# Attention transposes one turn after the scaling of their probabilities, in the turn of two interleaved scans that had no attention work

## What is computed

```python
s = (jnp.einsum('bqhd,bkhd->bhqk', qn_b, k_nope)
     + jnp.einsum('bqhd,bkd->bhqk', qr_b, k_rope))
p = jax.nn.softmax(s.astype(jnp.float32) * scale, axis=-1)
return jnp.einsum('bhqk,bkhd->bqhd', p.astype(v.dtype), v)
```

## Time and profile before

| | |
|---|---|
| median of 3 executions | 3255.03 us |
| profiled execution | 3253.55 us |
| its span | 3251.3 us |
| TensorE busy | 3132.6 us, 96% |
| VectorE, ScalarE, GpSimd busy | 64%, 41%, 29% |
| stretch with scans and attention | 531 to 1140 us |
| TensorE busy from 570 to 1128 us | 527.8 of 558.0 us |

### The profile page before, as it was taken

One profiled execution on the slowest core, in us unless ns is written; L12 is line 12 of the kernel. 1 busy time (PEld: TensorE's weight loads), 2 busy tenths in 40 slices (PEclk: granted clock), 3 DMA queues, 4 the chain that ended last, 5 costly groups with the idle time before them and its releaser, 6 DMA issues.

```text
span 3251.3 us, 62204 instructions
## 1 busy us (share of the span) xinstructions
PE 3132.6 (96%) x26688; PEld 2561.6 (79%) x26688; DVE 2084.1 (64%) x3018; ACT 1343.6 (41%) x2442; POOL 937.5 (29%) x810
## 2 busy tenths in 40 slices
PE   8999998999999988999999999999999999999998
PEld 8678776887788777787888888878677878888887
DVE  5263465666766665856999778752555575655686
ACT  4333334555555444533433344442332343333444
POOL 1232243222222142501576640000000025666100
PEclk9999999999999999999999999999999999999999
DMA  4241245112112122552222347422002312322753
GB/s 152 68 155 52 72 158 169 56 42 64 64 45 63 54 82 71 165 191 79 94 104 97 110 159 247 158 96 93 33 27 96 131 68 101 107 101 98 268 159 117
DMA packets 128018, 346.48 MB, mean 107 GB/s; under 512 B 15792, under 2 KB 19520, under 8 KB 124928
## 3 DMA queue, kind: packets, MB, share of 16 engines
q1 hardware_dynamic: 106592, 258.09, 23.8%
q0 software_dynamic: 21152, 84.42, 7.0%
HBM read 246.51 MB, written 95.94 MB: 105 GB/s over the span
## 4 chain that ended last, share of the span: by engine, by line
PE 84%; DVE 9%; ACT 4%; issue 2%; POOL 1%; DMA 1%; SPq 0%; DVEq 0%; ACTq 0%; POOLq 0%
PE ps L378 41%; PE ps L377 39%; PE ps L381 3%; DVE AR L387 2%; DVE X L387 2%; DVE SM L398 1%; DVE W L387 1%; ACT AR L384 1%; DVE WS L387 1%; DVE HT L391 0%; ACT WS L384 0%; ACT W L2379 0%; POOL AR L387 0%; ACT X L384 0%; DVE EX L387 0%
## 5 line engine op out<-in xcount | busy, mean ns | idle before, releaser
L387 DVE TENSOR_TENSOR WS<-W,WS 128x512 fp32r<-128x512 f32 (+1 forms) x284 | 341.7, 1204 | 245.8 <-ACT WS L384 245.6
L377 PE MATMUL ps<-HH,WS 128*128 128x512 f32 x1280 | 394.2, 389 | 0.0
L377 PE MATMUL ps<-TO,WS 128*128 128x512 f32 x1440 | 345.9, 389 | 0.0
L384 ACT ACTIVATE WS<-W 128x512 fp32r<-128x512 f32 (+1 forms) x284 | 210.0, 740 | 310.4 <-PE ps L378 165.2
L377 PEld LDWEIGHTS ps<-TO,WS 128*128 128x128 f32 x1440 | 270.3, 188 | 56.1
L377 PEld LDWEIGHTS ps<-HH,WS 128*128 128x128 f32 x1280 | 240.2, 188 | 49.9
L377 PE MATMUL ps<-HL,WS 128*128 128x512 f32 x640 | 249.0, 389 | 0.0
L378 PE MATMUL ps<-HH,WS 128*128 128x512 f32 (+1 forms) x736 | 230.3, 394 | 1.2 <-ACT HH L384 1.2
L377 PE MATMUL ps<-TO 128*128 128x512 f32 x936 | 226.8, 390 | 0.2 <-DVE TO L387 0.2
L378 PE MATMUL ps<-AR 64*64 64x64 f32 (+2 forms) x5440 | 202.8, 241 | 22.6 <-ACT AR L384 11.4
L384 ACT ACTIVATE X<-ps 128x512 f32<-128x512 f32 (+1 forms) x168 | 100.5, 598 | 284.5 <-PE ps L378 129.4
(11 more groups left out here) (387 smaller groups left out, 6530.5 us busy)
## 6 DMA issues: line engine op xcount, KB each, us to landing
AR_b<-h_d SPq DMA_DIRECT2D x154, 256.0 KB, 2.9
AR<-rw_d SPq DMA_DIRECT2D x104, 256.0 KB, 4.2
W<-in_w_fg SPq DMA_DIRECT2D x44, 512.0 KB, 3.8
W<-in_w_fu SPq DMA_DIRECT2D x44, 512.0 KB, 5.1
h_d<-FST POOLq DMA_DIRECT2D x20, 1024.0 KB, 4.4
x_d<-X POOLq DMA_DIRECT2D x24, 512.0 KB, 4.5
W<-in_w_tok SPq DMA_DIRECT2D x24, 512.0 KB, 4.0
rw_d<-X POOLq DMA_DIRECT2D x40, 256.0 KB, 3.3
```

The costliest lines, as they stand in the source:

```text
L377: return pe.e.matmul(o, l, r, start=start, stop=stop, skip_group_check=True)
L384: return e.e.activation(o, x, ACT.Copy)
L387: return e.e.tensor_tensor(o, x, y, op)
```

## The change

In the shared order of the attention's turns, the scaling gets a function of its own, `scale(i - 1)`, where the transposes stood; `transp(i - 1)` now stands in the next turn, behind `later(i)`. On TensorE that is the turn without attention work. ScalarE's copies of the transposes move with them, behind the exp of tile i. For the last tile the turns are arranged so that their number stays the same.

```diff
-        def att_steps(scores, transp, pv, load, later=lambda i: None, pieces=lambda *what: None):
+        def att_steps(scores, transp, pv, load, scale=lambda i: None, later=lambda i: None, pieces=lambda *what: None):
...
                     scores(i)
                 if 1 <= i <= 64:
-                    transp(i - 1)
-                yield
+                    scale(i - 1)
+                if i <= 64:
+                    yield
                 if i < 64:
                     later(i)
+                if 1 <= i <= 64:
+                    transp(i - 1)
+                if i <= 64:
                     yield
                 if i % 2 and i >= 3:
                     pv((i - 3) // 2)
...
-            return att_steps(skip, scale, skip, skip)
+            return att_steps(skip, skip, skip, skip, scale=scale)
```

## The result

The changed kernel took **3259.93 us** (median of 16 executions, 3255.69 to 3266.63), the kernel before 3255.02 us in as many (3250.55 to 3260.06). The ratio is 1.0017 with an interval of [1.0009, 1.0025]: 4.9 us slower, less than the 0.2% that I called no change, but no gain. It lies in the range, on the other side of the forecast of 3245. The profiled execution took 3263.16 us (span 3260.8), against 3253.55 before; it lies above the median of its kernel, so its gap to before, 9.6 us, is wider than that of the medians.

A forecast was written before the change was run, and what follows sets the result against it. TensorE, busy 96% of the span, was taken as the bound. Terms of -23.5 + 7.2 + 3 + 3 = -10.3 us took the profiled 3253.55 us to 3243.3; 3245 us was predicted for the median, range 3231 to 3264.

The forecast's parts named there:

- point 7: ScalarE's transpose copies move behind the exp and hold two of six ring banks: 3 us lost, bounds 0 and 15.
- Point 1: Transposes, moved out of the score turn, no longer wait for VectorE's scaling: 8.2 us off, bounds 0 and 8.2.
- points 1 to 4: The gains on TensorE in the interleaved scan and attention stage: 23.5 us together, between 4 and 30.
- Cover for the turn behind a quiet one: Transposes in the turn without attention hide its blocks' copies, ending 15 idles: 8.6 us off, bounds 0 and 8.6.
- Scores and exp: With 1 us more TensorE work in front, scores wait less for ACT's exp of the tile before: 2.7 us off.
- Restarts: Each TensorE stop also costs about 0.15 us of pipeline refill; about 27 stops ending saves 4 us.
- Changes of shape: 72 more switches of TensorE tile shape in the stage, 0.1 us each: 7.2 us lost, bounds 3 and 22.
- Less cover in the score turn: 1.5 us instead of 2.5 between its scan blocks and the quiet turn's lengthens stops: 3 us lost, bounds 0 and 8.
- Nothing elsewhere: VectorE, GpSimd and DMA queue keep their order, and work behind the stage is untouched: 0 us.
- rival B: The stops move: late copies stay late, half of points 2 to 4 is lost; -2 us, 3253, chance 0.25.
- rival A: Shape changes cost 22 us and bank waits 15, against 23.5 gained: +13 us, 3268, chance 0.15.
- the signs named as wrong: Scan blocks idle behind transpose copies or VectorE; weight-load idle without releaser up over 10 us; equally long stage, other wait names.

The follow-up runs named there:

- experiments 4 and 5: VectorE's scaling multiplication cut to a single column, in the changed kernel (4: 3248.49 us) and in the kernel before (5: 3240.2 us).
- 9 and 10: Kernel before plus one 64x64 matmul per tile, inside the scores (9: 3278.55 us) or ahead of them (10: 3262.96 us).
- Experiment 8: Changed kernel with ScalarE's copies of the transposes ahead of the exp, TensorE's order unchanged: 3260.22 us.
- experiment 7: Changed kernel with all eight transposes between the two scan blocks of the turn without attention, no longer behind both: 3340.46 us.

## Why the prediction was wrong

The sign failed by about 15 us: -10.3 was forecast, +4.9 measured. **The step that failed is point 7**, the bank waits, which were put at 3 us and measured 15.8 us in 20 stops, where the kernel before has 3.3 us in 3. Point 1 failed beside it: its waits went and came back elsewhere. Together they filled nearly all the room that points 1 to 4 had taken off. By its own steps:

1. *Waits for the scaling.* Right in that all 8.2 us went from the transposes; wrong in taking them as won. The late scaling came back as 7.7 us of stops of the quiet turn's scan blocks, which are gone when the scaling is left out (experiments 4 and 5). The bound of 0, "the waits reappear", was the case.
2. *Cover for the turn behind a quiet one.* The cover worked: at the same 15 matmuls the 8.6 us of stops fell to 2.2. But other stops came into those turns, and TensorE's stops behind a quiet turn rose from 13.7 to 16.9 us. In the place that the transposes had left, no uncovered copy shows: without the scaling the quiet turn's scan blocks have no stop of more than 0.15 us.
3. *Scores and exp.* These waits are gone (3.7 us in the rows before). The longest, of 2.02 us, has a successor of 2.02 us a little ahead of it, at 648.95, which waits for the same chain on ScalarE through a bank.
4. *Restarts.* 4 us were taken for about 27 stops that would end. As many others came, and no such gain can be told apart.
5. *Changes of shape.* The mechanism was right; 88 changes and not 72. By the pair of 9 and 10 one costs 0.16 us and not 0.1, which would be 14 us instead of 7.2; in the changed kernel itself 5 to 8 us are left for them. The bounds of 3 and 22 held it.
6. *Less cover in the score turn.* The two stops of 1.18 us that were to grow are gone from the quiet turn, and the transposes behind them stop instead (0.77 and 0.80 us, the same exponential). What grew there is point 1's 7.7 us. And nothing was charged for what stands behind some stops, a lower clock: 6 us more at the lower level in the means, some 2 us of time.
7. *ScalarE's queue and the banks.* **Failed by its size.** The waits behind the transposes' copies are 3.4 us in 7, as taken. But the prediction had also counted 22 takings of the transposes that wait for a result of the same turn, "23 before, then hidden by the scores", and charged nothing for losing that cover: they are 6.9 us in 10 stops. And scan blocks met the bank of the other scan's sums for 5.4 us in 3 (before, with the values, 3.3 in 3). The bound of 15 was reached. Experiment 8 shows that ScalarE's order doesn't matter, experiment 7 what one scan block less of distance costs.
8. *Nothing elsewhere.* Right: 8.8 of the 9.5 us by which the spans differ lie in the stage.

The time fits rival B, the stops move (0.25), and its "same"; and a part of its reason was right, VectorE coming behind at the quiet turn. But it is rival A's mechanism that did more, bank waits at the 15 us that it names, with the changes of shape below its 22 us. That the time stayed in the range is in part luck: A's banks and B's VectorE came together, and the gains of points 2 and 3 were real against them. No run takes the bank waits away, so what they cost by themselves, with the rest as it is, stays open. Of the signs named as wrong, all three appeared: scan blocks behind VectorE at the quiet turn's start, weight loads without a releaser up by 11 us, and other names at the waits of a stage no shorter.

## What to carry to other kernels

Work that moves into a hole brings its own waits along. Before moving it, list at the new place whom each buffer comes from and when that user lets go; a wait that the old neighbours hid (here 1.5 us of scores) is no longer hidden, though the trace of before shows nothing of it. A late producer that others share (VectorE here) only changes who waits for it. Delay and place are separate choices, and here the delay alone (one tile later, same neighbours) took 5.5 us off, while the place cost more than the delay gave. Where TensorE is the bound and work of different tile shapes is interleaved, count the changes of shape in program order, every pair of shapes, and keep equal shapes side by side.

## What was new about the hardware

- A change of tile shape costs 0.16 us of TensorE in the pair that differs in nothing else (experiments 9 and 10), and 0.06 to 0.15 us is what is left for one in the others. It is mostly booked as busy time, with no wait in the trace. Changes between 128x64 and 128x128 count as well: from a block's last 128x128 matmul to the next block's first start it takes 0.20 us, whether that is of 128x64 or 64x64, and 0.11 us within a block. From the 96-row scores to the 128-row transposes no such step is seen (0.23 us from start to start, as within the scores).
- Behind some stops of about 2 us, in an engine that is 96% busy, the clock lay at the lower level for 3.4 to 6.8 us (in the changed kernel at 651, 740 and 856 us); behind others, such as the stops of 2.02 and 2.22 us in the earlier trace rows, it did not. In the kernel before it fell once in the stage, behind the stop of 2.18 us at 738 us. So moving stops about may change the time even where their sum stays.
- VectorE's scaling, 128x1024 in place, usually takes 0.75 us, but up to 3.5 us. In all twelve runs that have it, every one longer than 0.8 us ends 0.55 to 0.62 us behind the end of a GpSimd instruction: 2.78 us near 736 us and 3.5 us near 847 us stand beside chains of GpSimd work of that length.
